# Dilated attention in a decoder block: scores of each head over its own 64 rows, and masks added by VectorE

## The chip, the cores and the metric

One Trainium2 chip, one of its NeuronCores. The metric is the device time of one launch of the whole program in microseconds (us). Engines are named as in the profile: PE (TensorE, matrix products; its weight loads are PEld), DVE (VectorE), ACT (ScalarE), POOL (GpSimd) and SP (SyncE, which here only issues DMAs).

## What is computed

One layer of a decoder over 2048 tokens of width 1024. It normalises the input, projects it once, and feeds three groups of heads: a gated linear attention, a recurrent branch, and the dilated attention that this case is about. Then come an output projection and a gated FFN with a convolution. The dilated attention has 6 heads of 64 channels. Each head attends in three patterns, with dilation 1, 4 and 16, and the patterns are then combined by their softmax denominators:

```python
DILATED_PATTERNS = ((128, 1), (512, 4), (2048, 16))
# in banded_causal_attention, for every block of 128 queries:
s = jnp.einsum('nbqhd,nbkhd->nbhqk', qb, kb).astype(jnp.float32) * (hd ** -0.5)
valid = (dist >= 0) & (dist <= span) & (blk * SWA_BLOCK + kj - SWA_BLOCK >= 0)
s = jnp.where(valid[None, :, None], s, -jnp.inf)
m = jnp.max(s, axis=-1, keepdims=True)
p = jnp.exp(s - m)
denom = jnp.sum(p, axis=-1, keepdims=True)
o = jnp.einsum('nbhqk,nbkhd->nbqhd', p / denom, vb.astype(jnp.float32))
lse = (m + jnp.log(denom))[..., 0].transpose(0, 1, 3, 2)
```

## The kernel before, in words

The program is a sequence of stages with a barrier of all engines between them: `input_projection`, `dilated_attention`, `gated_linear_attention`, `recurrent_and_patterns`, `output_projection`, `conv_ffn`. No stage begins before the last engine has left the one before it. The change lies in `dilated_attention` alone, and in the constants that it loads.

That stage first loads q, k and v (L436) and applies the rotary embedding (L468, L563, L566, L639). Then it works through 48 blocks of 128 queries. The first 32 are "wide": each has 256 keys (the previous and the current 128); blocks 0 to 15 read tokens at stride 1 and blocks 16 to 31 at stride 4. The last 16 are "single": 128 keys, at stride 16. The 6 heads are 3 groups (g = 0, 1, 2) of two heads; the 128 partitions of q, k and v of a group hold the 64 channels of one head and the 64 of the other.

Every engine has its own written order, and semaphores tie them together. For a block j:

- POOL copies the keys and values of block j, two blocks ahead, from the strided token layout into `k_s` and `v_s` (L482, L483, L486; for single blocks L485, L486). It waits until PE has used the buffer (`scores_ready`, `vt_done`).
- ACT stages the queries of block j + 2 (`stage_queries`, L520) twice: for each head of a pair the whole 128 rows are multiplied by a column of `head_scale` that is 1/8 on that head's 64 rows and 0 on the other 64. So a contraction over 128 rows gives one head's scores.
- PE, `scores`: for a group, two matmuls of the bf16 identity with the mask of the block (L662) write the masks to PSUM, and two f32 matmuls (L665) add the scores of the two heads. All of a group lies in one of three banks `s_bank[g]`, which is free again when ACT has taken the exponentials.
- DVE, `maxima` (L572): one reduction over both heads of the group gives the negated maxima `neg`.
- ACT, `exps` (L503): exp(score + neg) from PSUM to `probs`.
- PE, `turn_probs` (L678): four (single: two) transposes of the probabilities to `t_bank`. DVE copies them back for g = 0 and 2 (`turned_even`, L581), ACT for g = 1 (`turned_odd`, L512).
- PE, `sums` (L695, L696, single L698): the products with the values, and with a column of ones that gives the denominators, to `o_bank[slot]`. `turn_v` (L647) transposes the next values.
- DVE, `take_sums`: copies the sums (L587) and the maxima (L589) to `o_sb`, which SP stores (L445).

PE and DVE run one block deep as a pipeline; the order of PE within a block is

```python
scores(j, slot, wide, 0, False)
turn_probs(j - 1, 1 - slot, wide, 0, last_fresh)
scores(j, slot, wide, 1, False)
turn_probs(j - 1, 1 - slot, wide, 1, last_fresh)
sums(j - 1, 1 - slot, wide, 0)
turn_probs(j - 1, 1 - slot, wide, 2, last_fresh)
scores(j, slot, wide, 2, False)
sums(j - 1, 1 - slot, wide, 1)
turn_v(j, slot, wide)
sums(j - 1, 1 - slot, wide, 2)
```

and that of DVE is maxima 0, turned_even 0, maxima 1, turned_even 2, maxima 2, take_sums.

Of the kernel before, what the change touches and what calls it, by code (L numbers as in the profile page):

```python
# [9 lines left out]
BF16 = mybir.dt.bfloat16  # L10
# [354 lines left out]
def dilated_attention(nc, proj_t, rope, rotate, masks, ident, ident_bf, head_scales, o_scratch):  # L365

    with ExitStack() as ctx:
# [13 lines left out]
        mask = sb("mask", [P, PAIRED, 2 * SPAN], BF16)  # L381
        idf = sb("idf", [P, P])
        head_scale = sb("head_scale", [P, 2])
        idb = sb("idb", [P, P], BF16)
# [44 lines left out]
        def _(sp):  # L429
            sp.dma_start(rot_w[:, :], rotate).then_inc(rope_in, 16)  # L430
            sp.dma_start(cos_sin[:, :, :], rope).then_inc(rope_in, 16)
            sp.dma_start(head_scale[:, :], head_scales).then_inc(consts_in, 16)
# [5 lines left out]
            sp.dma_start(idb[:, :], ident_bf).then_inc(consts_in, 16)  # L438
# [12 lines left out]
        def unit_at(i, m):  # L451

            return bass.ds(i * (2 * NB) + m // GROUPS * NB, NB)

# [38 lines left out]
        def _(act):  # L493
# [3 lines left out]
            def exps(j, slot, wide, g, fresh):  # L497
# [33 lines left out]
            act.wait_ge(consts_in, 16 * 4)  # L531
# [17 lines left out]
        def _(dve):  # L549
# [33 lines left out]
            def take_sums(j, slot, uses):  # L583
# [3 lines left out]
                dve.tensor_copy(o_sb[:, slot, 0:NEG], o_bank[slot][:, 0:NEG]).then_inc(o_ready, 1)  # L587
# [26 lines left out]
            dve.wait_ge(v_ready, 2)  # L614
            start(0, 0, True)
            body(1, 1, True, None, True)
            body(2, 0, True, None)
            body(3, 1, True, 16)
            with dve.Fori(0, PAIRED // 2 - 2) as i:
                body(2 * i + 4, 0, True, 16 * (i + 1))  # L620
                body(2 * i + 5, 1, True, 16 * (i + 2))
            finish(PAIRED - 1, 1, True)
            start(PAIRED, 0, False)
            body(PAIRED + 1, 1, False, 16 * (PAIRED // 2))
            with dve.Fori(0, SINGLE // 2 - 1) as i:
                body(2 * i + (PAIRED + 2), 0, False, 16 * (i + PAIRED // 2))
                body(2 * i + (PAIRED + 3), 1, False, 16 * (i + (PAIRED // 2 + 1)))
# [3 lines left out]
        def _(pe):  # L631
# [9 lines left out]
            pe.wait_ge(consts_in, 16 * 4)  # L641
# [8 lines left out]
            def scores(j, slot, wide, g, fresh):  # L650
                width = (2 if wide else 1) * SPAN
                if g == 0:
                    pe.wait_ge(staged, staged_after(j, wide))
                    pe.wait_ge(q_staged, 2 * j + 2)
# [2071 lines left out]
```

## Time and profile before

| | |
|---|---|
| time, median of 3 runs | 2956.32 us (2954.72 to 2956.46) |
| span of the profiled execution | 2956.1 us (the page gives the span alone) |
| PE / DVE / ACT / POOL busy | 2584.5 / 1614.6 / 1069.4 / 752.2 us |
| first score matmul of the attention stage | 608.8 us from the start |
| last copy of its results by DVE | 933.7 us |
| its wide blocks, steady part | 623 to 839 us |
| its single blocks, steady part | 848 to 933 us |

How to read it: the attention stage's blocks take 325 of 2956 us. The stages are separated by barriers, so what the blocks of this stage take longer or shorter is seen one to one in the total. Inside the stage the blocks repeat with a period, and the profile is best read as one period of each kind: the start of a given instruction in one block, the start of the same in the next, and between them what each engine does and what it waits for. Times are microseconds; a row's first number is its start (from the start of the span) and the second how long the row lasts; "x4" is the number of instructions merged in it. A f32 matmul of the source shows as two steps (a weight load and a matmul each).

### The profile page before, as it was taken

The numbers are of one execution on the slowest core, as the hardware profiler recorded it, in microseconds if no ns is written. First come the engines' busy times: TensorE is split into PE (matmuls) and PEld (weight loads), VectorE is DVE, ScalarE is ACT, GpSimd is POOL, SyncE is SP. The second block draws the span as 40 slices with busy tenths as digits, with TensorE's granted clock in tenths as the row PEclk, the third lists the DMA queues.
The fourth block names the chain that finished last, engine by engine and source line by source line (L and its number), as shares of the span: only waits on it lengthen the run. The fifth ranks groups of instructions, "written<-read, shape, count | busy, mean of one in ns | idle before, by whom it ended". The sixth has DMA issues, their size and how long they took to land. (4 is left out here: it accounts for less than half of the span.)

```text
span 2956.1 us, 33825 instructions
## 1 busy us (share of the span) xinstructions
PE 2584.5 (87%) x12320; PEld 2103.6 (71%) x12320; DVE 1614.6 (55%) x1952; ACT 1069.4 (36%) x1683; POOL 752.2 (25%) x599
## 2 busy tenths in 40 slices
PE   7999999589985776227978999999998999998996
PEld 5788888379985555016857888887886888887884
DVE  7211111455555453883637777773556787774434
ACT  5000000046676431513215444442444444443342
POOL 4110000222331210731224333310303443430013
PEclk9999999899998555659989999999999999999998
DMA  4221211500003101427343222216462322223463
GB/s 149 86 75 71 75 71 64 201 17 28 28 32 115 39 26 49 157 104 242 129 184 131 86 86 85 80 65 232 149 235 75 122 100 82 76 92 121 167 235 110
DMA packets 117366, 315.47 MB, mean 107 GB/s; under 512 B 16944, under 2 KB 30016, under 8 KB 107008
## 3 DMA queue, kind: packets, MB, share of 16 engines
q1 hardware_dynamic: 117248, 313.95, 30.0%
q8 instruction: 68, 1.11, 0.2%
q14 instruction: 50, 0.41, 0.0%
HBM read 220.29 MB, written 93.62 MB: 106 GB/s over the span
## 5 line engine op out<-in xcount | busy, mean ns | idle before, releaser
L1898 PE MATMUL ff_bank<-ff_b_hi,ff_ring 128*128 128x512 f32 x1232 | 483.9, 393 | 36.9 <-DVE ff_ring L2443 15.1
L1899 PE MATMUL ff_bank<-ff_b_lo,ff_ring 128*128 128x512 f32 x1232 | 482.0, 391 | 0.0
L1900 PE MATMUL ff_bank<-ff_b_hi,ff_ring 128*128 128x512 f32 x1232 | 481.9, 391 | 0.0
L43 PE MATMUL ip_bank<-ip_x_hi,ip_w_hi 128*128 128x512 f32 x736 | 290.8, 395 | 19.2 <-DVE ip_x_lo L255 16.8
L1898 PEld LDWEIGHTS ff_bank<-ff_b_hi,ff_ring 128*128 128x128 f32 x1232 | 233.1, 189 | 90.9 <-issue 32.3
L1898 PE MATMUL ff_bank<-ff_a_hi,ff_w_hi 128*128 128x512 f32 x704 | 276.6, 393 | 15.6 <-DVE ff_a_lo L2495 15.5
L45 PE MATMUL ip_bank<-ip_x_hi,ip_w_lo 128*128 128x512 f32 x736 | 288.6, 392 | 0.0
L44 PE MATMUL ip_bank<-ip_x_lo,ip_w_hi 128*128 128x512 f32 x736 | 288.5, 392 | 0.0
L1899 PE MATMUL ff_bank<-ff_a_lo,ff_w_hi 128*128 128x512 f32 x704 | 275.6, 391 | 0.0
L1900 PE MATMUL ff_bank<-ff_a_hi,ff_w_lo 128*128 128x512 f32 x704 | 275.3, 391 | 0.0
L2481 DVE SCALAR_TENSOR_TENSOR ff_y<-ff_u,ff_conv_all,ff_y 128x1024 f32<-128x1024 f32 x176 | 240.2, 1365 | 63.2 <-ACT ff_y L2320 59.9
L1899 PEld LDWEIGHTS ff_bank<-ff_b_lo,ff_ring 128*128 128x128 f32 x1232 | 233.2, 189 | 48.5 <-issue 0.2
L1900 PEld LDWEIGHTS ff_bank<-ff_b_hi,ff_ring 128*128 128x128 f32 x1232 | 232.9, 189 | 48.7
L266 DVE TENSOR_TENSOR ip_staged<-ip_bank,ip_rstd 128x512 f32<-128x512 f32 x92 | 63.3, 691 | 362.7 <-PE ip_bank L45 362.6
L2443 DVE TENSOR_TENSOR ff_ring<-ff_raw,ff_ring 128x512 fp32r<-128x512 f32 x220 | 177.7, 809 | 56.8 <-ACT ff_ring L2301 56.8
L2493 DVE TENSOR_TENSOR ff_w_lo<-ff_w_raw,ff_w_hi 128x512 fp32r<-128x512 f32 x88 | 63.7, 724 | 243.5 <-ACT ff_w_hi L2334 243.5
L43 PEld LDWEIGHTS ip_bank<-ip_x_hi,ip_w_hi 128*128 128x128 f32 x736 | 139.7, 190 | 50.3 <-issue 13.2
L199 ACT ACTIVATE ip_w_hi<-ip_w_raw 128x1024 fp32r<-128x1024 f32 x23 | 24.4, 1060 | 402.9 <-PE ip_bank L45 389.4
L1898 PEld LDWEIGHTS ff_bank<-ff_a_hi,ff_w_hi 128*128 128x128 f32 x704 | 133.2, 189 | 45.6 <-DVE ff_a_lo L2495 17.6
L2334 ACT ACTIVATE ff_w_hi<-ff_w_raw 128x512 fp32r<-128x512 f32 x88 | 55.6, 632 | 302.8 <-PE ff_bank L1900 274.6
L44 PEld LDWEIGHTS ip_bank<-ip_x_lo,ip_w_hi 128*128 128x128 f32 x736 | 139.7, 190 | 30.2 <-issue 1.0
L45 PEld LDWEIGHTS ip_bank<-ip_x_hi,ip_w_lo 128*128 128x128 f32 x736 | 139.4, 189 | 29.2
(253 smaller groups left out, 4939.0 us busy)
## 6 DMA issues: line engine op xcount, KB each, us to landing
ff_raw<-in_slabs SPq DMA_DIRECT2D x44, 1024.0 KB, 4.8
ff_a_raw<-a_t SPq DMA_DIRECT2D x88, 512.0 KB, 4.1
proj_t<-ip_staged SPq DMA_DIRECT2D x92, 256.0 KB, 2.3
a_t<-ff_y SPq DMA_DIRECT2D x44, 512.0 KB, 2.7
ff_w_raw<-in_w_down SPq DMA_DIRECT2D x88, 256.0 KB, 2.7
ip_w_raw<-in_w_in SPq DMA_DIRECT2D x23, 512.0 KB, 3.3
o_scratch<-at_o_sb SPq DMA_DIRECT2D x48, 198.0 KB, 1.9
cb_rows<-o_scratch SPq DMA_DIRECT2D x24, 396.0 KB, 4.4
```

Of the source, the lines that this page charges most:

```text
L43: pe.matmul(out, w_hi[k], x_hi[k], start=(k == 0), stop=False)
L44: pe.matmul(out, w_hi[k], x_lo[k], start=False, stop=False)
L45: last = pe.matmul(out, w_lo[k], x_hi[k], start=False, stop=(k == n - 1))
L199: act.activation(w_hi[:, p, :, :], w_raw[:, :, :], ACT.Copy).then_inc(w_hi_ready, 1)
L266: dve.tensor_tensor(staged[:, bank % 2, :], banks[bank][:, :], rstd[:, blk(b)], ALU.mult).then_inc(bank_free, 1)
L1898: pe.matmul(out, w_hi, x_hi, start=first, stop=False, skip_group_check=resumed)
L1899: pe.matmul(out, w_hi, x_lo, start=False, stop=False, skip_group_check=resumed)
L1900: return pe.matmul(out, w_lo, x_hi, start=False, stop=last, skip_group_check=resumed)
L2334: act.activation(w_hi[n % 2][:, :], w_raw[n % 2][:, :], ACT.Copy).then_inc(d_hi_ready, 1)
L2443: dve.tensor_tensor(ring[:, M % RING, 1, :], source(half, m), ring[:, M % RING, 0, :].bitcast(F32), ALU.subtract).then_inc(w_lo_ready, 1)
L2481: dve.scalar_tensor_tensor(out=y[:, a, :], in0=u[:, a, t:t + HALF], scalar=conv_all[:, g, a, t:t + 1], in1=y[:, a, :], op0=ALU.mult, op1=A ...
L2493: dve.tensor_tensor(w_lo[n % 2][:, :], w_raw[n % 2][:, :], w_hi[n % 2][:, :].bitcast(F32), ALU.subtract).then_inc(d_lo_ready, 1)
```

## The change

- `scores`: no mask matmuls. The two heads' matmuls contract over 64 rows each (`k_s[rows]`, `q_s[rows]` with rows 0 to 63 and 64 to 127), and write to two different banks. The scores of a group now lie in a pair of banks, and there are two pairs (`score_at`), used in turn; a pair is free when DVE's extremum pass over it is done (`max_ready`), not when ACT is done.
- The queries are scaled by -1/8 and staged once (one ACT instruction of 384 columns in place of two). So the scores come out negated.
- `maxima`: DVE adds the mask (now f32, +1e30 where masked, two variants in place of 32) and takes the minimum in one `tensor_tensor_reduce` for each head, from PSUM and SBUF to a new buffer `masked` in SBUF. It also waits for ACT to have read the group's `masked` of the block before.
- `exps` reads `masked` from SBUF, with a scale of -1.
- `o_bank` is one bank in place of two, so the first sums of a block wait for DVE's copy of the block before.
- The loops over blocks are written out on DVE and PE.
- Fewer constants are loaded (no `head_scales`, no `ident_bf`, a mask of two variants).

```diff
-        mask = sb("mask", [P, PAIRED, 2 * SPAN], BF16)
+        mask = sb("mask", [P, 2, 2 * SPAN])
-        q_s = sb("q_s", [P, 2, GROUPS, 2, SPAN])
+        q_s = sb("q_s", [P, 2, GROUPS, SPAN])
+        masked = sb("masked", [P, GROUPS, 2, 2 * SPAN])
-        s_bank = [bank(f"s{i}") for i in range(GROUPS)]
+        s_bank = [bank(f"s{i}") for i in range(4)]
-        o_bank = [bank(f"o{i}") for i in range(2)]
+        o_bank = bank("o")
...
+        def score_at(j, g, hh, width):
+
+            return s_bank[2 * ((GROUPS * j + g) % 2) + hh][:, 0:width]
...
-                    ins = act.activation(probs[:, g, hh * width:(hh + 1) * width], s_bank[g][:, hh * width:(hh + 1) * width],
-                                         ACT.Exp, bias=neg_at(slot, hh, g))
+                    ins = act.activation(probs[:, g, hh * width:(hh + 1) * width], masked[:, g, hh, 0:width],
+                                         ACT.Exp, bias=neg_at(slot, hh, g), scale=-1.0)
...
-                for hh in range(2):
-                    act.activation(q_s[:, j % 2, :, hh, :], tokens(0, dil * SPAN * b + r, dil), ACT.Copy,
-                                   scale=head_scale[:, hh:hh + 1]).then_inc(q_staged, 1)
+                act.activation(q_s[:, j % 2, :, :], tokens(0, dil * SPAN * b + r, dil), ACT.Copy,
+                               scale=-HD ** -0.5).then_inc(q_staged, 1)
...
+                at = mask[:, min(blocks[j][2], 1), :] if wide else mask[:, 0, SPAN:]
                 dve.wait_ge(scores_ready, GROUPS * j + (g + 1))
-                dve.tensor_reduce(neg[:, slot, 2 * g:2 * g + 2],
-                                  s_bank[g][:, 0:2 * width].rearrange("p (h k) -> p h k", h=2), AX.X, ALU.max,
-                                  negate=True).then_inc(max_ready, 1)
+                if j:
+                    dve.wait_ge(probs_ready, GROUPS * (j - 1) + (g + 1))
+                for hh in range(2):
+                    ins = dve.tensor_tensor_reduce(masked[:, g, hh, 0:width], score_at(j, g, hh, width), at, 1.0, 0.0, ALU.add, ALU.min,
+                                                   accum_out=neg[:, slot, 2 * g + hh:2 * g + hh + 1])
+                ins.then_inc(max_ready, 1)
...
-                if not fresh:
-                    pe.wait_ge(probs_ready, GROUPS * j + (g - 2))
-                if wide:
-                    at = mask[:, bass.ds(j, 1), :] if not isinstance(j, int) else mask[:, j:j + 1, :]
-                else:
-                    at = mask[:, 1:2, SPAN:2 * SPAN]
+                if GROUPS * j + g >= 2:
+                    pe.wait_ge(max_ready, GROUPS * j + g - 1)
                 for hh in range(2):
-                    pe.matmul(s_bank[g][:, hh * width:(hh + 1) * width], idb[:, :], at.rearrange("p o k -> p (o k)"),
-                              start=(hh == 0), stop=False, skip_group_check=True)
-                for hh in range(2):
-                    ins = pe.matmul(s_bank[g][:, hh * width:(hh + 1) * width], q_s[:, slot, g, hh, :],
-                                    k_s[:, slot, g, 0:width], start=False, stop=(hh == 1), skip_group_check=True)
+                    rows = slice(HD * hh, HD * (hh + 1))
+                    ins = pe.matmul(score_at(j, g, hh, width), q_s[rows, slot, g, :], k_s[rows, slot, g, 0:width], start=True, stop=True)
                 ins.then_inc(scores_ready, 1)
...
-                    pe.wait_ge(o_ready, 2 * j + 1)
+                    pe.wait_ge(o_ready, 2 * j + 3)
```

How the instructions stand. On DVE, a wide block in the steady part: before (L571, L585, L601: register and wait instructions of the loop).

```order
L572 TENSOR_REDUCE at_neg<-at_s 128x2
L581 COPY at_probs_t<-at_t 128x512
L571 REGISTER_ALU
L572 TENSOR_REDUCE at_neg<-at_s 128x2
L581 COPY at_probs_t<-at_t 128x512
L571 REGISTER_ALU
L572 TENSOR_REDUCE at_neg<-at_s 128x2
L585 ISA
L587 COPY at_o_sb<-at_o 128x390
L589 COPY at_o_sb<-at_neg 128x6
```

The same block on DVE after the change (line numbers are those of the changed kernel, L574 the `tensor_tensor_reduce`, L583 the copy of the transposes, L589 and L591 the copies of sums and minima; the row "at_neg 128x1" is an instruction that writes the accumulator out).

```order
L574 ISA at_masked,at_neg<-at_s,at_mask 128x256
L574 ISA at_neg 128x1
L574 ISA at_masked,at_neg<-at_s,at_mask 128x256
L574 ISA at_neg 128x1
L583 COPY at_probs_t<-at_t 128x512
L574 ISA at_masked,at_neg<-at_s,at_mask 128x256
L574 ISA at_neg 128x1
L574 ISA at_masked,at_neg<-at_s,at_mask 128x256
L574 ISA at_neg 128x1
L583 COPY at_probs_t<-at_t 128x512
```

Each reduction has become four instructions, ahead of the copies that stood behind it; the third group (four more) and the two copies to `at_o_sb` follow.

On PE, the first part of a wide block before (L656, L671: registers of the loop):

```order
L662 MATMUL at_s<-at_mask,at_idb 128x256 x2
L665 MATMUL at_s<-at_k_s,at_q_s 128x256 x2
L671 REGISTER_ALU
L678 MATMUL at_t<-at_idf,at_probs 128x128 x4
L656 REGISTER_ALU
L662 MATMUL at_s<-at_mask,at_idb 128x256 x2
L665 MATMUL at_s<-at_k_s,at_q_s 128x256 x2
L671 REGISTER_ALU
L678 MATMUL at_t<-at_idf,at_probs 128x128 x4
```

and after (L656 the scores, L668 the transposes, L685 and L686 the sums):

```order
L656 MATMUL at_s<-at_k_s,at_q_s 128x256 x2
L668 MATMUL at_t<-at_idf,at_probs 128x128 x4
L656 MATMUL at_s<-at_k_s,at_q_s 128x256 x2
L668 MATMUL at_t<-at_idf,at_probs 128x128 x4
L685 MATMUL at_o<-at_v_tok,at_probs_t 128x65
L686 MATMUL at_o<-at_v_tok,at_probs_t 128x65
```

The two mask matmuls of each group are gone, and every group of score matmuls still stands between matmuls that use all 128 rows.

## Rows read from the trace of the kernel before

**Rows 1.** busy time by stretch: PE, PEld, DVE, ACT, POOL; granted clock; DMA share; GB/s

```profile
623.00:839.00 216.00, 216.00 (x1659) 202.44 (x1658) 121.30 (x205) 141.76 (x292) 59.52 (x87) 1.00 0.07 27
848.00:933.00 85.00, 70.86 (x646) 66.70 (x644) 51.09 (x113) 62.92 (x157) 23.28 (x28) 1.00 0.11 39
1100.00:1150.00 50.00, 41.84 (x262) 31.61 (x260) 17.56 (x37) 11.63 (x24) 2.93 (x2) 0.50 0.00 1
```

**Rows 2.** timeline, PE in one wide block of stride 1: start, duration, instruction

```profile
703.01 0.50 PE L647 MATMUL at_v<-at_idf,at_v_s 128*128 128x128 f32 x3
...
704.18 0.38 PE L662 MATMUL at_s<-at_mask,at_idb 128*128 x2
...
705.27 0.60 PE L678 MATMUL at_t<-at_idf,at_probs 128*128 128x128 f32 x4
...
705.71 0.38 PE L662 MATMUL at_s<-at_mask,at_idb 128*128 x2
...
707.23 0.34 PE L695 MATMUL at_o<-at_v_tok,at_probs_t 128*128 128x65 f32 x2
...
708.07 0.61 PE L678 MATMUL at_t<-at_idf,at_probs 128*128 128x128 f32 x4
...
710.43 0.50 PE L647 MATMUL at_v<-at_idf,at_v_s 128*128 128x128 f32 x3
```

**Rows 3.** the same timeline, DVE and ACT

```profile
705.47 0.69 DVE L572 TENSOR_REDUCE at_neg<-at_s 128x2 f32<-128x512 f32 x1 [0.37 <-PE at_s L665]
...
706.08 0.68 DVE L581 COPY at_probs_t<-at_t 128x512 f32<-128x512 f32 x1
...
707.72 0.84 ACT L503 ACTIVATE at_probs<-at_s,at_neg 128x256 f32<-128x256 f32 x2 [0.68 <-DVE at_neg L572]
...
708.45 0.60 ACT L512 ACTIVATE at_probs_t<-at_t 128x512 f32<-128x512 f32 x1
```

**Rows 4.** timeline, DVE in a wide block of stride 4

```profile
779.17 0.44 DVE L589 COPY at_o_sb<-at_neg 128x6 f32<-128x6 f32 x1
```

**Rows 5.** timeline, one single block (stride 16)

```profile
883.25 0.50 PE L647 MATMUL at_v<-at_idf,at_v_s 128*128 128x128 f32 x3
...
884.67 0.90 POOL L486 COPY at_v_s<-at_qkv 128x384 f32<-128x384 f32 x1
...
884.73 0.86 DVE L589 COPY at_o_sb<-at_neg 128x6 f32<-128x6 f32 x1
...
885.72 0.42 DVE L572 TENSOR_REDUCE at_neg<-at_s 128x2 f32<-128x256 f32 x1
886.06 0.41 DVE L581 COPY at_probs_t<-at_t 128x256 f32<-128x256 f32 x1
...
886.71 0.63 PE L698 MATMUL at_o<-at_v_tok,at_probs_t 128*128 128x65 f32 x4 [0.91 <-DVE at_probs_t L581]
...
888.41 0.50 PE L647 MATMUL at_v<-at_idf,at_v_s 128*128 128x128 f32 x3
```

**Rows 6.** timeline, PE in the gated linear attention: small products on different tiles

```profile
1014.51 0.37 PE L903 MATMUL gl_bank_s<-gl_q_mid,gl_k_mid 48*64 48x64 f32 x1
1014.52 0.37 PE L905 MATMUL gl_bank_s<-gl_q_mid,gl_k_mid 48*64 48x64 f32 x1
```

**Rows 7.** timeline, PE in the same stage: full rows and 48 rows in turn

```profile
1107.26 0.74 PE L930 MATMUL gl_bank_o<-gl_v_tok,gl_scores 128*128 128x96 f32 x2
1107.93 0.74 PE L931 MATMUL gl_bank_o<-gl_state,gl_q_start 48*128 48x96 f32 x2
```

**Rows 8.** timeline, two short DVE instructions in a later stage

```profile
1208.47 0.17 DVE L1396 TENSOR_SCALAR lr_sp<-lr_sp 128x2 f32<-128x2 f32 x1
1208.55 0.16 DVE L1397 TENSOR_SCALAR lr_sp<-lr_sp 128x2 f32<-128x2 f32 x1
```

**Rows 9.** the page, costliest groups: mean ns of one ScalarE copy from SBUF

```profile
L2334 ACT ACTIVATE ff_w_hi<-ff_w_raw 128x512 fp32r<-128x512 f32 x88 | 55.6, 632 | 302.8 <-PE ff_bank L1900 274.6
```

**Rows 10.** timeline, PE in the first block of the stage

```profile
611.32 1.92 PE L665 MATMUL at_s<-at_k_s,at_q_s 128*128 128x256 f32 x4
```

More of the change, by code:

```diff
@@ L362, in attention_blocks, with dilated_attention @@
                 yield pat, r, b
-def dilated_attention(nc, proj_t, rope, rotate, masks, ident, ident_bf, head_scales, o_scratch):
+def dilated_attention(nc, proj_t, rope, rotate, masks, ident, o_scratch):
     with ExitStack() as ctx:
@@ L586, in take_sums @@
                 dve.wait_ge(o_done, j + 1)
[L587 removed]
+                dve.tensor_copy(o_sb[:, slot, 0:NEG], o_bank[:, 0:NEG]).then_inc(o_ready, 1)
                 dve.wait_ge(max_ready, GROUPS * (j + 1))
@@ L614, in _ @@
             dve.wait_ge(v_ready, 2)
+            dve.wait_ge(consts_in, 16 * 2)
             start(0, 0, True)
[L616 to L621, printed above, removed]
+            for j in range(1, PAIRED):
+                body(j, j % 2, True, 16 * ((j - 1) // 2) if j > 2 else None, j == 1)
             finish(PAIRED - 1, 1, True)
             start(PAIRED, 0, False)
[L624 to L627, printed above, removed]
+            for j in range(PAIRED + 1, PAIRED + SINGLE):
+                body(j, j % 2, False, 16 * ((j - 1) // 2))
             finish(PAIRED + SINGLE - 1, 1, False)
@@ L640, in _ @@
                                   start=True, stop=True).then_inc(rotated, 1)
-            pe.wait_ge(consts_in, 16 * 4)
+            pe.wait_ge(consts_in, 16 * 2)
             pe.wait_ge(times_sin, 2 + 2 * UNITS)
@@ L689, in sums @@
                     pe.wait_ge(v_ready, j + 3)
-                    pe.wait_ge(o_ready, 2 * j + 1)
+                    pe.wait_ge(o_ready, 2 * j + 3)
                 for hh in range(2):
                     h = 2 * g + hh
-                    out = o_bank[slot][:, h * OW:(h + 1) * OW]
+                    out = o_bank[:, h * OW:(h + 1) * OW]
                     if wide:
@@ L728, in _ @@
             body(1, 1, True, True)
-            with pe.Fori(0, PAIRED // 2 - 1) as i:
-                body(2 * i + 2, 0, True)
-                body(2 * i + 3, 1, True)
+            for j in range(2, PAIRED):
+                body(j, j % 2, True)
             finish(PAIRED - 1, 1, True)
@@ L734, in _ @@
             body(PAIRED + 1, 1, False)
-            with pe.Fori(0, SINGLE // 2 - 1) as i:
-                body(2 * i + (PAIRED + 2), 0, False)
-                body(2 * i + (PAIRED + 3), 1, False)
+            for j in range(PAIRED + 2, PAIRED + SINGLE):
+                body(j, j % 2, False)
             finish(PAIRED + SINGLE - 1, 1, False)
@@ L1591, in shape_constants @@
     k = np.arange(SPAN)[None, :]
-    masks = np.zeros((P, PAIRED, 2 * SPAN), np.float32)
-    for j, (pat, r, b) in enumerate(attention_blocks()):
-        if j < PAIRED:
-            masks[:, j, :SPAN] = np.where((k >= q) & (b > 0), 0.0, -1e30)
-            masks[:, j, SPAN:] = np.where(k <= q, 0.0, -1e30)
-    ident = np.eye(P, dtype=np.float32)
-    head_scales = np.zeros((P, 2), np.float32)
-    for head in range(2):
-        head_scales[head * HD:(head + 1) * HD, head] = HD ** -0.5
-    return {"head_scales": head_scales, "rope": rope, "rotate": rotate, "masks": bf16_bits(masks), "ident": ident,
-            "ident_bf": bf16_bits(ident)}
+    masks = np.zeros((P, 2, 2 * SPAN), np.float32)
+    for later in range(2):
+        masks[:, later, :SPAN] = np.where((k >= q) & (later > 0), 0.0, 1e30)
+        masks[:, later, SPAN:] = np.where(k <= q, 0.0, 1e30)
+    return {"rope": rope, "rotate": rotate, "masks": masks, "ident": np.eye(P, dtype=np.float32)}
 FFN = 2816
@@ L2659, in program @@
         input_projection(nc, t["x_t"], t["norm_mix"], t["w_in"], proj_t)
-        dilated_attention(nc, proj_t, t["rope"], t["rotate"], t["masks"].bitcast(BF16), t["ident"], t["ident_bf"].bitcast(BF16), t["head_scales"], o_scratch)
+        dilated_attention(nc, proj_t, t["rope"], t["rotate"], t["masks"], t["ident"], o_scratch)
         gated_linear_attention(nc, proj_t, t["gla_w_gate"], t["gla_b_gate"], t["starts"], t["causal"], t["ident"], t["gla_norm"], mix_t)
```

10 lines of the change are left out of this document (1 added, 9 removed).

## The prediction

> **What bounds the kernel now.** I read the busy time of stretches first, to find how full each engine is in the attention stage, then the timeline of one block of each kind. The stage stands alone between barriers, so only its own chain counts, and every microsecond of it is one of the total.
>
> In the wide blocks TensorE is busy for all of the 216.00 us, at a granted clock of 1.00 (2.4 GHz); in the single blocks for 70.86 of 85 us [rows 1]. One wide block, from turn_v to turn_v, takes 710.43 - 703.01 = 7.42 us [rows 2]. Its parts add up without a gap: a group of scores with masks 705.27 - 704.18 = 1.09 us, four transposes 705.71 - 705.27 = 0.44, the sums of a group 708.07 - 707.23 = 0.84 (eight steps of 0.105). Three groups of scores are 3.27 us; all else is 7.42 - 3.27 = 4.15 us. So the wide blocks are bound by TensorE. Under it lies a chain that is nearly as long: scores end, VectorE reduces (705.47) and 0.61 us later copies transposes (706.08), reduces again, ScalarE takes exponentials (707.72, for 0.73 until the next begins) and turns its share of the probabilities (708.45, 0.60 long) [rows 3]; about 0.25 us after that the second sums may start. Where PE waits least, this chain decides.
>
> In wide blocks of stride 4 VectorE's little copy of the maxima takes 0.44 us and ends at 779.61 [rows 4]. A single block takes 888.41 - 883.25 = 5.16 us. There the copy of the maxima lasts 0.86 us in place of about 0.16: it starts at 884.73, 0.06 us after GpSimd has begun a copy of 0.90 us, and both end at about the same time. The reduction follows at 885.72, the copy of transposes 0.34 us later, and TensorE has waited 0.91 us for that copy when its sums start at 886.71 [rows 5]. So single blocks are bound by a chain through GpSimd's copy and VectorE, not by TensorE.
>
> **The change, part by part.** (1) *Mask matmuls gone.* Two bf16 steps before each group of scores. A score step is taken as 0.2175 us (twice the 0.109 of a 128-column step from the 0.44 for four), four of them 0.87, so the masks are 1.09 - 0.87 = 0.22 us a group.
>
> (2) *Row tiles.* Nothing in the trace shows this form at full clock. Bounds: the two heads overlap fully (0.44 us a group) or not at all (0.87). Each f32 matmul is two steps on the same rows, issued in order, so the third step may begin with the second and the fourth must follow it: three steps, 0.65 us. I take that. Small products on different tiles do start within 0.01 us of each other [rows 6].
>
 A group is then 0.65 + 0.40 = 1.05 us, and TensorE's sum is 4.15 + 3 x 1.05 = 7.30 us a wide block. Nearly all that is saved is given back.
>
> (4) *VectorE.* One reduction over a group becomes two masked passes, each with an instruction that writes the accumulator out. A pass over 256 columns is 0.42 us, 0.34 to the next start (the reduction of 256 [rows 5]). The read-out isn't in the trace. Bounds: free (0.34 a head in all), or a full short instruction behind a full pass (0.42 + 0.16 = 0.58). Two short instructions of a later stage start 0.08 us apart, and last 0.17 [rows 8]. I take the pass in full, since the accumulator is complete only at its end, and 0.06: 0.48 a head, 0.96 a group in place of 0.61. For 128 columns 0.133 less: 0.35 a head, 0.70 in place of 0.34. Two groups lie on the chain of every block.
>
> (5) *Exponentials from SBUF.* A ScalarE copy of 512 columns from SBUF takes 0.632 us [rows 9], from PSUM 0.60 [rows 3]: 0.03 an instruction, 0.07 on the chain.
>
> (6) *Queries staged once.* ScalarE is not on the chain of wide blocks; in single blocks it was close to it (its second staging ends just before the first exponentials). Nothing by itself; it only leaves VectorE's chain as the one bound.
>
> (7) *One sums bank, two pairs of score banks, a wait for `masked`.* The copy of the sums starts as soon as the last sums end, and is over (0.56) long before the next first sums, which stand behind two groups of scores and two of transposes (2.2 us). The other two waits look at work two or three groups back. Nothing, unless VectorE falls 1 us behind.
>
> (8) *Written-out loops, fewer constants.* The loop's register work is hidden in front of waits, and the constants landed long before use. Nothing.
>
> (9) *First blocks.* At half clock four score steps take 1.92 us [rows 10]; the start has three groups in a row. About 0.5 us a group is saved: -1.5 us.
>
> **The sums.** Wide, stride 1, from turn_v: sums 0.33 to 1.17, switch to 1.37, scores end at 2.18 (0.65 and a tail of 0.16), VectorE begins at 2.22; 0.96, then the copy's 0.61, then 0.96 gives 4.75 and the end at 4.83; exponentials 0.80; turning 0.60; 0.25: the second sums start at 6.5, and turn_v follows after 0.84, at 7.34. TensorE's own sum is 7.30. So 7.35 against 7.42, over 15 blocks: -1 us. Stride 4: VectorE is free only 2.37 us after turn_v (779.61 against 777.24) [rows 4], so 0.1 later: 7.46, over 16 blocks: +0.6. Single: VectorE's reduction starts 2.47 us after turn_v as before [rows 5]; from there 0.70 + 0.34 + 0.70 + 0.08 to the second minima, exponentials 0.54 + 0.07, turning 0.40, 0.25, sums 0.39: 5.94 against 5.16. In the 13 blocks that still have GpSimd's copies beside them: +10. Sum: -1 + 0.6 + 10 - 1.5 = +8 us. The profiled span is 2956.1 us, which is 0.2 below the median of the runs; I forecast **2964 us**, slower by 0.27%. A measurement of this kernel can tell about 0.2%, 6 us, from no change.
>
> **The rules of the skill.** The Trainium skill, "TensorE: Matmul & The Clock Gate", section "Measured speedup vs the span model", has tiles of different rows end one after another by some 4 ns, whatever their number; by it a group's scores would take 0.44 us, TensorE's sum would be 6.67 and stride-1 blocks 7.13, 3 us less in all. The rows here show only starts of small products. The Trainium skill, "Vector Engine (DVE) Microarchitecture Reference", section 5.2, gives each instruction some 75 ns beside its columns; by it a pass with its read-out would be 0.42 us in place of 0.48, which is the first rival.
>
> **The rivals.** *No change:* the read-out costs only the 0.08 us between the starts of short instructions [rows 8], on top of 0.34: 0.42 a head. The chain has four of them: -0.24 a block. Stride 1 stays at TensorE's 7.30 (-1.8), stride 4 falls to 7.22 (-3.2), single to 5.70 (+7), start -1.5: **2957 us**. For it: every other VectorE instruction overlaps its follower by 0.08. Chance 0.30. (The Trainium skill's 75 ns, above, would give the same.)
>
> *Faster:* the read-out vanishes under the next pass, at 0.34 a head (the value that is decisive is about 0.37). The chain is 0.56 shorter: stride 4 6.9 (-8), single 5.38 (+3), stride 1 7.30 (-1.8), start -1.5: **2948 us**. If the copy of the minima also slips ahead of GpSimd's, which it misses by 0.06 us [rows 5], single blocks lose a further 0.7. Against it: an accumulator can't be read before the last column. Chance 0.15.
>
> *Slower, TensorE stays the bound:* the switch costs 0.30, or the two heads don't overlap at all (0.87): the change then doesn't do what it says. A group is 1.25 to 1.27 us, a wide block 7.9 to 8.0, 31 blocks x 0.53 = +16, with the single blocks' +10 and -1.5: **2981 us**. For it: the switch was measured at half clock, and its tail may be no shorter at full. It decides from a group of 1.10 us up, where TensorE's sum passes the chain. The Trainium skill, "TensorEngine Tiling (Array Packing)", section "Key Properties", says that a change of mode drains the engine, without a price. Chance 0.20.
>
> The forecast has 0.35, with its own range 2958 to 2970.
>
> **The numbers.** The range takes in half of the fast case and nearly all of the slow one: 2948 to 2982. Faster by over 0.2%: 0.16. Within: 0.34 (most of the no-change case, a part of the forecast). Slower: 0.50.
>
> **What would show it.** On TensorE: the distance from the first score step to the first transpose of a group (0.85 if (2) holds), and from the last transpose to the scores (0.3 in place of 0.11). On VectorE: two rows to each head, together 0.48 between starts. In wide blocks idle PE under 0.2 us a block; in single blocks a period of 5.9 us with PE waiting 1.2 us or more for the copy of transposes, and the copy of the minima still at 0.85. I am wrong if the single blocks' period falls, if wide blocks pass 7.6, or if PE's clock leaves 1.00.

## The result and the profile after

| | before | after |
|---|---|---|
| device time, median (12 runs each, same chips) | 2954.77 us | 2960.64 us |
| lowest to highest | 2950.42 to 2959.32 | 2952.03 to 2966.00 |
| ratio, 95% interval | | 1.0019 [1.0010, 1.0027] |
| profiled execution: its time | not given | 2963.28 us |
| its span | 2956.1 us | 2961.5 us |
| its mean granted clock | 0.912 | 0.894 |

The change costs about 6 us, 0.19%. That is 3 us from the forecast and on its side of zero, but the forecast is right for the wrong reason: its terms for the row tiles, for VectorE and for the single blocks were off, and the cost comes from the one thing that it took as constant, TensorE's clock. That the two sums come out so close is luck.

**Wide blocks became faster, by far more than forecast.** First the timeline of PE in the first of the longer wide blocks (start, duration, instruction), which answers to [rows 2]. It is counted with stride 4 here: GpSimd works two blocks ahead and copies its first keys of stride 4 beside it, at 0.88 to 0.91 us a copy where those of stride 1 took 0.51.

```profile
703.60 0.50 PE L644 MATMUL at_v<-at_idf,at_v_s 128*128 128x128 f32 x3
...
704.87 0.70 PE L656 MATMUL at_s<-at_k_s,at_q_s 64*128 64x256 f32 x4
705.50 0.66 PE L668 MATMUL at_t<-at_idf,at_probs 128*128 128x128 f32 x4
706.09 0.70 PE L656 MATMUL at_s<-at_k_s,at_q_s 64*128 64x256 f32 x4
...
708.39 0.61 PE L668 MATMUL at_t<-at_idf,at_probs 128*128 128x128 f32 x4
708.92 0.70 PE L656 MATMUL at_s<-at_k_s,at_q_s 64*128 64x256 f32 x4
709.56 0.44 PE L685 MATMUL at_o<-at_v_tok,at_probs_t 128*128 128x65 f32 x2
...
710.50 0.50 PE L644 MATMUL at_v<-at_idf,at_v_s 128*128 128x128 f32 x3
```

From the first score step to the product behind the group it is 705.50 - 704.87 = 0.63 us, with the switch back to full rows in it; four transposes with the switch to half rows behind them are 708.92 - 708.39 = 0.53 in one place and 706.09 - 705.50 = 0.59 in another, against 0.44 in [rows 2]. With the smaller of the two, a group costs 0.63 + 0.09 = 0.72 us, not 1.09 as before and not 1.05 as forecast. The block takes 6.90 us.

VectorE in the same block, which answers to [rows 3, 4]:

```profile
705.52 0.45 DVE L591 COPY at_o_sb<-at_neg 128x6 f32<-128x6 f32 x1
706.01 0.42 DVE L574 CUSTOM_DVE_ANT_0 at_masked<-at_s,at_mask 128x256 f32<-128x256 f32 x1
706.36 0.08 DVE L574 DVE_READ_ACCUMULATOR2_ANT at_neg<- 128x1 f32 x1
706.36 0.42 DVE L574 CUSTOM_DVE_ANT_0 at_masked<-at_s,at_mask 128x256 f32<-128x256 f32 x1
706.70 0.08 DVE L574 DVE_READ_ACCUMULATOR2_ANT at_neg<- 128x1 f32 x1
706.70 0.69 DVE L583 COPY at_probs_t<-at_t 128x512 f32<-128x512 f32 x1
```

The read-out of the accumulator starts in the same moment as the next pass. A head costs 0.345 us from start to start: the read-out is free, as the "faster" rival had it. The copy of the maxima still takes 0.45 us beside GpSimd's copies of stride 4, and 0.16 in the blocks before: the same 0.29 us by which those blocks are longer below.

The copy of the sums (L589) marks each block. Of after, its first and last rows in three steady stretches, 9, 16 and 12 blocks apart:

```profile
645.55 0.57 DVE L589 COPY at_o_sb<-at_o 128x390 f32<-128x390 f32 x1 [1.49 <-PE at_o L686]
...
705.04 0.57 DVE L589 COPY at_o_sb<-at_o 128x390 f32<-128x390 f32 x1 [1.49 <-PE at_o L686]
...
815.40 0.57 DVE L589 COPY at_o_sb<-at_o 128x390 f32<-128x390 f32 x1 [1.49 <-PE at_o L686]
...
847.38 0.56 DVE L589 COPY at_o_sb<-at_o 128x390 f32<-128x390 f32 x1 [1.98 <-PE at_o L688]
...
931.78 0.56 DVE L589 COPY at_o_sb<-at_o 128x390 f32<-128x390 f32 x1 [1.98 <-PE at_o L688]
```

Stride 1: (705.04 - 645.55)/9 = 6.61 us. Stride 4: (815.40 - 705.04)/16 = 6.90. Single: (931.78 - 847.38)/12 = 7.03, where before it was 5.16 [rows 5].

**Single blocks lost it all again, because the clock fell.** Stretches of PE alone; the columns are length, busy time (matmuls), granted clock, DMA share and GB/s, here and in all such stretches below:

```profile
835.00:836.00 1.00, 0.83 (x7) 1.00 0.03 8
836.00:837.00 1.00, 0.38 (x3) 1.00 0.46 174
837.00:838.00 1.00, 0.93 (x9) 1.00 0.08 29
838.00:839.00 1.00, 0.97 (x6) 0.69 0.00 0
839.00:840.00 1.00, 1.00 (x7) 0.50 0.00 0
```

A longer stretch, of the part at the lower clock:

```profile
880.00:890.00 10.00, 10.00 (x50) 0.50 0.05 20
```

At 838 us, in the third single block, the granted clock goes from 1.00 to 0.50 (2.4 to 1.2 GHz) and stays there for the rest of the stage, though PE is now busy for all of the time. In before it is 1.00 all through these blocks, with PE busy for 8.19 of 10 us. At half clock TensorE's own sum is the bound: 7.03 us a block.

The account of the stage, from the first score product to the last copy of sums: before 608.80 to 933.65, after 606.82 to 936.65, so +5.0 us. It is -2.1 up to the first copy of sums, -19.2 over the next 30 steps from copy to copy (222.8 to 203.6 us), +26.3 from there to the last copy, nearly all of it single blocks (87.6 to 113.9). The forecast had -1.5, about 0 and +10.

### The profile page after: what moved, and what is told of

Read it like the earlier page. It is cut to its first block and busy times, and to the rows that moved or that the text cites. A ratio compares the mean times of both kernels' runs of the same rounds, so it can differ in the third digit from the quotient of the medians.

```text
span 2961.5 us, 33037 instructions
## 1 busy us (share of the span) xinstructions
PE 2600.9 (88%) x12032; PEld 2067.2 (70%) x12032; DVE 1617.4 (55%) x2384; ACT 1043.4 (35%) x1635; POOL 751.2 (25%) x599
```

## The experiments

What was open: whether the clock is the whole loss, what makes it fall, what keeps it down, what the row tiles are worth by themselves, and what would bind the single blocks at full clock. Each run was timed beside before on its own chip; before's median there was 2953.94 us for the first four below, 2954.00 for the next four edits (before without masks, full rows from the seventh block, the first five blocks, the copy moved) and 2954.68 for the rest. Where "one run" is said, the effect is read from the trace, and the time only supports it.

### Fuller single blocks with row tiles

```
-                for c in range(4 if wide else 2):
+                for c in range(4 if wide else 2) if wide or g != 1 else [0, 1] * 3:
```

> Edit: in the single blocks the two transposes of group 1 are issued three times over (the same data written again to the same place), so that TensorE has fewer idle stretches where the single blocks begin; about 0.44 us of work more in each of them. Theory A (the single blocks lose because TensorE's granted clock fell to 0.50 after its idle stretches at their start): the clock holds 1.00, a single period of 4.7 to 5.0 us instead of 7.03, the kernel 2936 to 2942 us. Theory B (my forecast: the chain over VectorE and GpSimd sets the single blocks, whatever the clock): the clock may hold, the period stays above 5.8 us, the kernel at least 2950 us. Theory C (the clock falls because the score products have half the rows, idle or not): the clock still falls to 0.50, the period grows to about 7.9 us for the added products at half clock, the kernel about 2967 us.

2935.33 us, ratio 0.9935 [0.9918, 0.9951]. More work on TensorE made the kernel 25 us faster than the change: the clock stays at 1.00 to the stage's end. So the clock is the loss, and theory C in its bare form (row tiles always lose it) falls. That it held is no accident of one run: the mean clock of the four runs was 0.910 to 0.913, that of the change's twelve 0.893 to 0.902. Theory A was right on the clock, but both forecasts of the period missed. A single block, timeline of PE, POOL and DVE:

```profile
859.94 0.88 POOL L486 COPY at_v_s<-at_qkv 128x384 f32<-128x384 f32 x1
860.02 0.83 DVE L591 COPY at_o_sb<-at_neg 128x6 f32<-128x6 f32 x1
...
860.88 0.29 DVE L574 CUSTOM_DVE_ANT_0 at_masked<-at_s,at_mask 128x128 f32<-128x128 f32 x1
...
861.31 0.42 DVE L583 COPY at_probs_t<-at_t 128x256 f32<-128x256 f32 x1
...
861.78 0.66 PE L688 MATMUL at_o<-at_v_tok,at_probs_t 128*128 128x65 f32 x4 [0.34 <-DVE at_probs_t L583]
...
863.69 0.50 PE L644 MATMUL at_v<-at_idf,at_v_s 128*128 128x128 f32 x3
...
868.82 0.50 PE L644 MATMUL at_v<-at_idf,at_v_s 128*128 128x128 f32 x3
```

The period is 868.82 - 863.69 = 5.13 us, before's. The chain is the one that the forecast named: the copy of the maxima blocked for 0.83 us behind GpSimd, then VectorE, then TensorE's sums, which waited for L583. But two passes take 0.43 us (860.88 to 861.31), not 0.70.

### Full rows in the single blocks

```
-                act.activation(q_s[:, j % 2, :, :], tokens(...), ACT.Copy, scale=-HD ** -0.5).then_inc(q_staged, 1)
+                if j < PAIRED:
+                    act.activation(q_s[:, j % 2, :, :], tokens(...), ACT.Copy, scale=-HD ** -0.5).then_inc(q_staged, 2)
+                else:
+                    for hh in range(2):
+                        act.activation(q_z[:, j % 2, :, hh, :], tokens(...), ACT.Copy, scale=head_scale[:, hh:hh + 1]).then_inc(q_staged, 1)
...
+                    else:
+                        ins = pe.matmul(score_at(j, g, hh, width), q_z[:, slot, g, hh, :], k_s[:, slot, g, 0:width], start=True, stop=True)
```

> Edit: the single blocks' scores contract over all 128 rows again (queries staged twice, the other head's rows zero), VectorE still adds the masks; wide blocks as in the change. Score group 0.44 us instead of about 0.35 plus its switches. Theory C (half the rows let the clock fall): the clock holds 1.00 and the single period is 4.7 to 5.1 us, the kernel 2936 to 2944 us. Theory A (idle at the start of the single blocks lets it fall): the idle stretches of TensorE there stay at nearly their length, so the clock falls all the same, a single period of 7.0 to 7.4 us, the kernel 2959 to 2966 us. Theory B: 5.9 us at full clock, 2950 us.

2936.86 us, ratio 0.9945 [0.9928, 0.9961]: row tiles in the wide blocks alone are 24 us better than the change. The outcome is theory C's, with a period of 5.17 us, just above its range. Here TensorE idles longer than in the change, and the clock holds all the same (mean 0.910 in all four runs). Stretches of PE at the passage to single blocks:

```profile
831.00:832.00 1.00, 0.30 (x3) 1.00 0.00 0
832.00:833.00 1.00, 0.00 (x0) 1.00 0.00 0
```

So theory A in its bare form (idle time alone) falls too. From 870 to 900 us PE was busy for 23.71 us here and for 27.43 in the run before. Over full rows the clock held with little work, with row tiles it held with more.

### No row tiles at all

The same with `if False` for both conditions: queries staged twice for every block.

> Edit: all blocks' scores contract over all 128 rows as before the change, and VectorE adds the masks: the change without its row tiles. Wide blocks: TensorE's sum is 4.15 us of the rest and three groups of four score steps at 0.87 us, 6.76 us, with no switches; if row tiles earned only the 0.63 against 0.87 us less their switches, the wide stride is 6.7 to 7.0 us, within 0.3 us of the change's 6.61 and 6.90. If the gain of the wide blocks is mainly the row tiles' (my step 2), the stride goes back to 7.1 us or more. Single blocks: theory A gives a fallen clock and 7.0 to 7.4 us, or a held one with 4.8 to 5.1 us if TensorE's idle stretches shrink at their start; theory C gives a held clock, 4.8 to 5.1 us. Kernel: 2961 to 2970 us with a fallen clock, 2938 to 2948 with a held one.

2943.80 us, ratio 0.9964 [0.9952, 0.9977]. From copy to copy of the sums, wide blocks take 6.92 us (stride 1) and 6.93 (stride 4). All of the change but the row tiles and the single staging, the moved masks above all, thus brings 7.42 - 6.92 = 0.50 us a block; row tiles add 0.31 in stride 1 and 0.03 in stride 4, where VectorE binds. Most of the gain in the wide blocks is the masks' (TensorE's sum without them is 4.15 + 3 x 0.87 = 6.76, so 0.16 us of the block is in gaps that have nothing to do with row tiles), which the forecast had at 0.66 a block and then let the row tiles eat up. In this run the clock fell at the start of the single blocks, behind a stretch of idle, and came back. Its stretches of PE, at the fall and at the return:

```profile
838.00:839.00 1.00, 0.00 (x0) 1.00 0.00 0
...
840.00:841.00 1.00, 1.00 (x6) 0.50 0.00 0
```
```profile
844.00:845.00 1.00, 1.00 (x10) 1.00 0.45 163
```

### Both heads on the same rows

```
-                    rows = slice(HD * hh, HD * (hh + 1))
+                    rows = slice(0, HD)
```

> Edit: the second head's scores are taken from the first head's 64 rows (so the second head's output is the first head's scores on its own values), and the two heads' products no longer lie in different row tiles. If the row tiles run beside each other, as I took it, a wide group's score products now follow one another at 0.22 us each: from the first score product to the product behind the group 1.0 to 1.1 us instead of 0.63. If the 0.63 us comes from something else (a shorter product with half the rows), it stays at 0.63. In the first case the wide stride grows by about 3 x 0.4 us where TensorE binds, to 7.3 to 7.8 us, and the kernel by 12 to 30 us.

3027.18 us (one run). The same two steps of the wide block as above, timeline of PE:

```profile
701.78 1.13 PE L656 MATMUL at_s<-at_k_s,at_q_s 64*128 64x256 f32 x4
702.84 0.66 PE L668 MATMUL at_t<-at_idf,at_probs 128*128 128x128 f32 x4
```

1.06 us instead of 0.63: the tiles overlap, and by 0.43 us, which is two of the four steps. So the overlap is complete as far as these rows tell, and my "third step" (0.65 us a group) does not exist. By that, 0.63 is 0.44 of products and 0.19 for the way back to full rows; 1.06 less the 0.87 of four steps in a row gives 0.19 too. The Trainium skill, "TensorE: Matmul & The Clock Gate", section "Measured speedup vs the span model", gives a pack of tiles the time of one product and some 4 ns for each further tile. This pair of runs agrees with it. The wide block took 7.84 us, just above the expected 7.3 to 7.8. The kernel's time is far above the 12 to 30 us expected, because the clock was low for longer: it rose only at 635 us (613 in the change), though PE was busy for all of the time from 607 us on, and it fell in the passage to the single blocks, which then took 8.29 us each. PE had been busy for 19.25 of the 20 us up to 870 us and for 7.00 of the 8 from 866 to 874. Stretches of PE:

```profile
872.00:874.00 2.00, 1.75 (x13) 1.00 0.28 101
874.00:875.00 1.00, 1.00 (x7) 0.87 0.00 0
875.00:876.00 1.00, 1.00 (x5) 0.50 0.00 0
```

### Before, without the single blocks' masks

The two mask products of L662 are issued under `if wide:` alone, so this kernel leaves out the causal mask of the single blocks.

> Edit: the kernel before without the mask matmuls of the single blocks (the causal mask of those blocks is left out), so TensorE has 0.66 us less to do in each, all of it still over 128 rows. Theory C (full rows hold the clock, row-tile products don't): the clock stays at 1.00 through the single blocks although TensorE idles longer, the period 5.1 us, the kernel 2950 to 2957 us. Theory A (idle alone lets it fall): with more idle than the change has (about 1.5 us in each block), the clock falls to 0.50, the period about 6.5 to 7 us, the kernel 2970 us or more.

2955.41 us (one run). The steady single blocks keep the clock at 1.00 with PE busy for only 7.67 of 10 us. Yet at the passage it had fallen (0.50 at 855 us, behind a whole idle microsecond), which theory C did not expect, and was back at 858. The period is 5.02 us: 0.66 us less work on TensorE brought 0.1, so TensorE does not bind there.

### Full rows from a late single block on

The second experiment with `j < PAIRED + 6` for both conditions, then with `j < PAIRED + 11`.

> Edit: the change, but from the seventh single block on the scores contract over all 128 rows (queries staged twice with zeros). The clock falls to 0.50 in the third single block as in the change. Theory C (what the row-tile products do not give the engine in work is what keeps the clock down): the granted clock goes back to 1.00 within some 5 us of the seventh single block (it took 4 us in the run without row tiles), and the remaining nine blocks take 5.15 us each; the kernel about 2943 to 2948 us. Rival (once fallen, it stays until the stage's end whatever TensorE does): it stays at 0.50 with periods of 7.3 to 7.6 us, the kernel 2963 us or more.

2934.00 us (one run). The expectation failed at its premise: with row tiles and, on TensorE, the very program of the change up to there, the clock had not fallen by the seventh single block. Its row-tiled single blocks took 5.13 to 5.18 us, which is the change's chain at full clock: no longer than before's 5.16. A stretch of PE in them:

```profile
850.00:860.00 10.00, 8.03 (x66) 1.00 0.11 41
```

Its PE rows up to 838 us differ from the change's by tenths of a microsecond (it idles from 831.3 to 832.1, not from 832.1 to 832.9). So the fall is not fixed by the program. The test was repeated five blocks later.

> Edit: as the run with full rows from the seventh single block on, in which the clock had not fallen by then, but from the twelfth single block on. The clock should have fallen before (in all runs of the change the mean clock says that it fell within about seven blocks). Theory C (what the row-tile products do not give the engine in work keeps the clock down): it goes back to 1.00 within about 5 us of the first full-row blocks and the last four periods are 5.15 us; the kernel 2944 to 2957 us, by the block in which it fell. Rival (once fallen it stays): 7.0 us or more to the end, the kernel 2955 to 2968 us.

2949.70 us (one run). Now the clock had fallen in the third single block. PE's timeline where the full-row products begin, and its stretches:

```profile
894.26 1.16 PE L668 MATMUL at_s<-at_k_s,at_q_z 128*128 128x128 f32 x4
```
```profile
880.00:890.00 10.00, 10.00 (x48) 0.50 0.11 41
...
896.00:897.00 1.00, 1.00 (x7) 0.50 0.55 203
897.00:898.00 1.00, 1.00 (x9) 0.70 0.07 16
```

From 840 to 890 us PE was busy for 10.00 of each 10 us with row tiles and the clock stayed at 0.50. The first score products over full rows start at 894.26; the clock rises at 897 to 898 us, some 3.5 us later, to 1.00, and the next periods are 5.14 to 5.22 us. On TensorE nothing else changed at that point. This shows that the row-tiled score products keep the clock down in the single blocks. It does not tell their half rows from the switches that come with them, which no run separates. Nor do row tiles rule out a rise: in the wide blocks of the change the clock rose to 1.00 at 613 us, 7 us after the first scores.

### More work in the first five single blocks alone

```
+                for c in [0, 1] * 3 if g == 1 and PAIRED <= j < PAIRED + 5 else range(4 if wide else 2):
```

> Edit: the change, with the repeated transposes of group 1 in the first five single blocks alone. Theory A' (only the idle stretches at the passage from wide to single blocks matter, and the steady single blocks would keep the clock): the clock stays at 1.00 to the end, the kernel 2936 us or a little less. Theory C' (the single blocks with row tiles have too little work for the clock in their steady run as well, 3.8 to 4.2 us of 5.1): the clock falls to 0.50 within one to three blocks after the last repeated transposes, at 860 to 875 us, periods of 7.03 us from there, the kernel 2950 to 2956 us.

2949.47 us (one run), as theory C' had it. The clock held while the repeated transposes lasted (to 850 us) and fell at 863 us, in the second block after that. Stretches of PE:

```profile
861.00:862.00 1.00, 0.71 (x6) 1.00 0.55 203
862.00:863.00 1.00, 0.89 (x9) 1.00 0.08 16
863.00:864.00 1.00, 1.00 (x9) 0.68 0.03 8
```

It is therefore not only the passage from wide to single blocks. Steady single blocks with row tiles, busy for 8.0 to 8.3 of 10 us, lost the clock here and kept it in the run with full rows from the seventh block on; with full rows and 7.67 of 10 none lost it in its steady run.

### The change once more

> Edit: none, the changed kernel once more. If the point at which the clock falls is not fixed by the program, it lies in another single block than the third, each block later being worth 7.03 - 5.14 = 1.9 us; the time is then 2935 us and 1.9 us for each single block after the fall. If the program fixes it, it falls at 838 us from the start again, and the time is 2960 to 2964 us.

2962.33 us (one run); it fell at 838 us again. Of the four runs that have this program up to the seventh single block, three fell in the third block and one not before the seventh. The second outcome of the expectation is what this run shows, the sixth experiment speaks for the first. In the 12 timed runs of the change the time goes with the mean clock (2952.03 us at 0.902, 2966.00 at 0.894), as falls in different blocks would make it; only one of the twelve has a trace.

### The copy of the maxima first

In `take_sums`, VectorE copies the maxima before it waits for the sums; TensorE's wait for the bank is one count higher.

```
-                dve.wait_ge(o_done, j + 1)
-                dve.tensor_copy(o_sb[:, slot, 0:NEG], o_bank[:, 0:NEG]).then_inc(o_ready, 1)
                 dve.wait_ge(max_ready, GROUPS * (j + 1))
                 dve.tensor_copy(o_sb[:, slot, NEG:ROW], neg[:, slot, :]).then_inc(o_ready, 1)
+                dve.wait_ge(o_done, j + 1)
+                dve.tensor_copy(o_sb[:, slot, 0:NEG], o_bank[:, 0:NEG]).then_inc(o_ready, 1)
...
-                    pe.wait_ge(o_ready, 2 * j + 3)
+                    pe.wait_ge(o_ready, 2 * j + 4)
```

> Edit: the change, with VectorE's two copies to the outgoing tile in the other order: the small copy of the maxima first, before it waits for the sums, where GpSimd's copies don't run. It takes that copy (0.83 us in single blocks at full clock, 0.44 in wide blocks of stride 4) off the way to the next block's first pass. Wide blocks of stride 4: 6.61 to 6.75 us in place of 6.90, 16 blocks: -2.5 to -4.6 us. Single blocks at full clock would take about 4.5 us, with TensorE busy for 4.2 of it. If idle stretches decide on the clock, it holds now and the kernel takes about 2922 to 2930 us. If the row-tile products are what lets it fall, it falls here too (it fell with both heads in the same rows at 0.96 busy): period 7.0 us as before, since at half clock TensorE itself binds, the kernel 2955 to 2958 us.

**2918.85 us, ratio 0.9876 [0.9859, 0.9892]**: 35 us under before, and the best version found. It is a little better than the better of the two expected outcomes. Wide blocks take 6.60 us in both strides. A single block, timeline, and under it a stretch of PE:

```profile
862.05 0.50 PE L644 MATMUL at_v<-at_idf,at_v_s 128*128 128x128 f32 x3
...
866.27 0.17 DVE L589 COPY at_o_sb<-at_neg 128x6 f32<-128x6 f32 x1
...
866.39 0.50 PE L644 MATMUL at_v<-at_idf,at_v_s 128*128 128x128 f32 x3
```
```profile
850.00:860.00 10.00, 9.79 (x78) 1.00 0.12 43
```

The copy takes 0.17 us where GpSimd is idle, against 0.83 beside it. The period is 4.34 us. The Trainium skill, "SBUF — State Buffer", section "Who interferes with whom", says that VectorE's copies of some forms need the pair of ports that it shares with GpSimd, and that whichever is issued first has it for a whole instruction while the other is blocked. The two durations agree with it. The clock held at 1.00 here. Since another run with row tiles lost it while nearly as busy (both heads on the same rows), that it always holds isn't shown; four runs of four had a mean clock of 0.910 to 0.912.

### The same with full rows, and the same on the kernel before

> Edit: the small copy of the maxima first, and single blocks with scores over all 128 rows. It tells whether row tiles are worth anything in the single blocks once VectorE's chain is shorter. A single block with row tiles took 4.34 us with TensorE 0.98 busy. With full rows its sum is about the same (four steps 0.44 us against 0.49 and the switches): if TensorE's sum binds, 4.1 to 4.4 us; but ScalarE stages the queries twice (16.97 of 20 us busy at 5.16 us a block, 4.38 us of work a block), so it may bind at 4.4 to 4.7. Kernel 2917 to 2924 us. If the clock falls here and not in the run with row tiles, theory C is wrong.

2930.55 us (2924.02 to 2935.62), ratio 0.9919 [0.9903, 0.9936]. The single block is back at 5.18 us. The expectation's 4.1 to 4.7 was wrong, since it added up ScalarE's work and not its chain. Timeline of ScalarE and VectorE in a single block:

```profile
865.91 1.82 ACT L527 ACTIVATE at_q_z<-at_qkv,at_head_scale 128x384 f32<-128x384 f32 x2
...
866.49 0.08 DVE L583 DVE_READ_ACCUMULATOR2_ANT at_neg<- 128x1 f32 x1
...
867.63 1.26 ACT L506 ACTIVATE at_probs<-at_masked,at_neg 128x128 f32<-128x128 f32 x4
```

VectorE's minima of the group were ready at 866.57 (866.49 and 0.08), but the exponentials stood behind the second staging of queries until 867.63. The clock fell here too, at 826 us behind a stretch with no work, and was back at 833 with full rows. That goes against theory C as the expectation puts it: full rows didn't prevent the fall, but in all four runs in which the clock had fallen and the single blocks used full rows, it came back.

> Edit: the kernel before with VectorE's small copy of the maxima first. It tells what the swap is worth without the change. Wide blocks stay at TensorE's sum, 7.42 us. Single blocks: 0.5 to 0.7 us less of 5.14, 4.45 to 4.65 us, where ScalarE's double staging may bind: -7 to -10 us, the kernel 2944 to 2948 us. If it were to gain 20 us or more, the swap and not the change would carry most of the 35 us of the run with both.

2952.86 us, ratio 0.9995 [0.9985, 1.0004]: nothing that can be told, where 7 to 10 us were expected. Its single blocks take 5.03 us, not 4.45 to 4.65, and again the exponentials start only as the double staging ends. Timeline of ScalarE:

```profile
862.48 1.80 ACT L520 ACTIVATE at_q_s<-at_qkv,at_head_scale 128x384 f32<-128x384 f32 x2
864.19 1.12 ACT L503 ACTIVATE at_probs<-at_s,at_neg 128x128 f32<-128x128 f32 x4
```

Two chains of nearly one length run beside each other in the single blocks of before: VectorE's with the blocked copy (5.13 alone) and ScalarE's with the double staging (5.03 to 5.18 alone). Taking away either gives nothing or 0.1; the change takes away the second, the swap the first, and both together give 4.34.

## Why the prediction was right and wrong

- **Total.** Forecast 2964 us, range 2948 to 2982; measured 2960.64. The nearness is luck: two errors cancel. The sum of +8 was made of +10 in single blocks from a chain that did not lengthen. In the runs it is -21 in the wide part and the first blocks, and +26 from the clock. The single blocks' chain is worth 0 against before (5.13 to 5.18 at full clock, 5.16 before).
- **(1) Masks gone.** Of 3 x 0.22 = 0.66 us a block, 0.50 came through in the run without row tiles; the size is about right.
- **(2) Row tiles, 0.65 us a group.** The first step that failed. It is 0.44, the lower bound: heads overlap in full. The argument from issue order had no row behind it, and the rule of the Trainium skill, "TensorE: Matmul & The Clock Gate", section "Measured speedup vs the span model", which I gave beside it, was right.
- **(3) Switch, 0.20 each way.** 0.19 back to full rows holds; on the way to half rows it is 0.09 in one place, below the lower bound of 0.12, and 0.15 in another. A group is 0.72 us at the least and TensorE's sum 4.15 + 3 x 0.72 = 6.31. The block took 6.60 with PE never idle in the records. Of the other 0.29 us, 0.06 is the longer of the two switches and 0.10 lies in the sums behind the third group (710.50 - 709.56 = 0.94 us for 0.84). The rest isn't explained; the run without row tiles, which has no switches, is 0.16 over its sum as well.
- **(4) VectorE, 0.48 and 0.35 us a head.** The second step that failed: 0.345 and 0.215, so the two passes of a single block's group take 0.43 us and not 0.70. "The accumulator is complete only at its end" was true and cost nothing, since the next pass doesn't wait. With (2) and (3) it explains the wide blocks. The "faster" rival, given 0.15, was right in its read-out. Its stride-4 period of 6.9 us came true, but by its own working it could not have: it kept TensorE's sum of 7.30, which bounds both strides. By that sum stride 4 would have been 7.30 and the rival 2954 us, not 2948; the 7.22 of the "no change" rival has the same slip. A smaller one: stride 4 starts VectorE 2.37 - 2.22 = 0.15 us later, not 0.1, which is under 1 us in all.
- **(5)** held: exponentials take 0.501 us in place of 0.470.
- **(6) Queries staged once, "nothing by itself".** True in this change, and true only because VectorE's chain is as long; with the copy moved, single staging and row tiles together are worth 5.18 - 4.34 = 0.84 us a block, and ScalarE's rows put it down to the staging.
- **(7), (8)** nothing: no row of the runs shows a cost, though none tests them alone. **(9)** -2.1 us against -1.5.
- **The third of my own signs of error came in.** "I am wrong if PE's clock leaves 1.00" was written and no rival had it. Before's rows showed the clock at 1.00 in single blocks with idle of 0.9 us a block, and I took that for safe in any form. The missing rival was: single blocks at half clock, 7.0 us a block, +26 us in all, with the wide blocks at -20.

## What to carry to other kernels

When a change leaves TensorE less to do or halves the rows that its products use, the granted clock is a term of the sum: price the affected stretch at 0.50 as a rival of its own, and look there first in the result. Where a block is bound by a chain, look for a second chain of the same length before valuing the removal of one; here either alone gave at most 0.1 us a block and both 0.8. A small instruction that gets blocked by another engine can often be moved to a moment when that engine is idle: one swap of two copies was worth 42 us on top of this change, some 25 of them by the clock (2960.64 - 2935.33, from the run with fuller blocks).

## What was not expected of the hardware

- At the lower clock TensorE was busy for 10.00 of every 10 us of the single blocks with 64-row products among its work, for some 90 us, and the clock did not rise. With 128-row score products it rose some 3.5 us after the first of them (one run by design; three more times, within 3 to 7 us of the fall, at the passage to single blocks). In wide blocks it did rise with 64-row products: 7 us after the first scores in the change, 29 us after them with both heads on the same rows.
- The same instructions lost the clock in the third single block in three profiled runs and kept it for six blocks in a fourth. What decides between them stays open.
- Switching from 128 to 64 rows costs 0.09 to 0.15 us and back 0.19 at full clock, and an accumulator's read-out of 0.08 us lies wholly under the next pass.
